# Up projection of a hybrid encoder: low and high activations as one 512-column moving operand

## What is computed

```python
h = rmsnorm(x, ffn_norm_g[l])
up = causal_dwconv(h @ w_ffn_up[l], ffn_dw_w[l], ffn_dw_b[l])   # 1024 -> 2 x 2816, width 3
gt, val = jnp.split(up, 2, axis=-1)
x = x + (jax.nn.silu(gt) * val) @ w_ffn_down[l]                 # 2816 -> 1024
...
return rmsnorm(x, final_norm_g)
```

## Time and profile before

| | us |
|---|---|
| median of 3 runs | 819.56 |
| lowest, highest | 819.24, 820.25 |
| profiled execution, its time | 820.79 |
| its span, first to last instruction | 819.0 |

### The profile page before, as it was taken

How to read it: one execution, slowest core, us unless ns; L and a number is a source line. 1 busy time by engine, 2 the same in 40 slices (tenths; PEclk the granted TensorE clock), 3 DMA queues, 4 the chain that set the end, 5 groups by cost and what they waited for, 6 DMA issues and landing times.

```text
span 819.0 us, 16096 instructions
## 1 busy us (share of the span) xinstructions
PE 803.6 (98%) x6554; PEld 777.2 (95%) x6554; DVE 585.7 (72%) x1157; ACT 520.6 (64%) x862; POOL 455.2 (56%) x139
## 2 busy tenths in 40 slices
PE   8999999999999999999999999999999999999997
PEld 8999988899999999999999999998999999999996
DVE  5799998583468875666669999885634786766655
ACT  6766798774566564555577577887546664545545
POOL 6898787787822223222288987877787024222330
PEclk9999999999999999999999999999999999999999
DMA  7654444444545555555545544444464456555441
GB/s 285 217 200 155 155 156 155 145 164 160 202 155 183 202 181 197 173 197 174 187 154 178 183 159 161 151 149 139 172 229 161 164 192 206 199 167 200 164 145 52
DMA packets 21385, 142.76 MB, mean 174 GB/s; under 512 B 2496, under 2 KB 3008, under 8 KB 4672
## 3 DMA queue, kind: packets, MB, share of 16 engines
q1 hardware_dynamic: 20736, 140.69, 49.9%
q10 hardware_dynamic: 576, 1.04, 0.3%
HBM read 140.68 MB, written 1.05 MB: 173 GB/s over the span
## 4 chain that ended last, share of the span: by engine, by line
PE 83%; ACT 7%; DVE 6%; issue 1%; DMA 1%; POOL 1%; SPq 0%; DVEq 0%; ACTq 0%
PE pu L1058 22%; PE pu L1060 22%; PE pu L1059 22%; ACT whi L319 2%; DVE pc L769 2%; DVE wlo L914 1%; PE ps L1318 1%; PE ps L1319 1%; PE ps L1320 1%; DMA x<-in_x_t 1%; PE ps L1060 1%; PE ps L1059 1%; PE ps L1058 1%; PE ps L1170 1%; ACT probs L496 1%
## 5 line engine op out<-in xcount | busy, mean ns | idle before, releaser
L261 POOL TENSOR_TENSOR wlo<-raw,whi 128x2048 fp32r<-128x2048 f32 x86 | 397.2, 4623 | 333.0 <-ACT whi L319 332.7
L1058 PE MATMUL pu<-uh,whi 128*128 128x256 f32 x880 | 249.8, 284 | 1.6 <-POOL wlo L261 1.4
L319 ACT ACTIVATE whi<-raw 128x2048 fp32r<-128x2048 f32 x129 | 245.6, 1905 | 7.9 <-PE pu L1060 7.3
L1060 PE MATMUL pu<-uh,wlo 128*128 128x256 f32 x880 | 249.0, 283 | 0.0
L1059 PE MATMUL pu<-ul,whi 128*128 128x256 f32 x880 | 249.0, 283 | 0.0
L1058 PE MATMUL pu<-hh,whi 128*128 128x256 f32 x704 | 201.7, 286 | 2.2 <-POOL wlo L261 1.4
L1060 PE MATMUL pu<-hh,wlo 128*128 128x256 f32 x704 | 199.1, 283 | 0.0
L1059 PE MATMUL pu<-hl,whi 128*128 128x256 f32 x704 | 199.1, 283 | 0.0
L1058 PEld LDWEIGHTS pu<-uh,whi 128*128 128x128 f32 x880 | 168.8, 192 | 2.4 <-issue 1.9
L1059 PEld LDWEIGHTS pu<-ul,whi 128*128 128x128 f32 x880 | 168.9, 192 | 0.4
L1060 PEld LDWEIGHTS pu<-uh,wlo 128*128 128x128 f32 x880 | 168.8, 192 | 0.0
(11 more groups left out here) (237 smaller groups left out, 1173.8 us busy)
## 6 DMA issues: line engine op xcount, KB each, us to landing
raw<-in_weights SPq DMA_DIRECT2D x130, 1024.0 KB, 4.9
raw<-in_weights SPq DMA_DIRECT2D x3, 512.0 KB, 8.9
out_y<-qk SPq DMA_DIRECT2D x3, 256.0 KB, 2.4
x<-in_x_t SPq DMA_DIRECT2D x2, 256.0 KB, 5.0
raw<-in_weights SPq DMA_DIRECT2D x2, 256.0 KB, 3.9
x<-in_x_t SPq DMA_DIRECT2D x1, 512.0 KB, 8.2
gate<-in_final_g ACTq DMA_DIRECT2D x1, 512.0 KB, 4.0
out_y<-qk ACTq DMA_DIRECT2D x1, 256.0 KB, 2.9
```

The costliest lines, as they stand in the source:

```text
L261: nc.gpsimd.tensor_tensor(wlo[s][:, :], raw[s][:, :], whi[s][:, :].bitcast(f32), ALU.subtract).then_inc(lo_ready[s], 1)
L319: A(whi[s][:, :], raw[s][:, :], ACT.Copy).then_inc(hi_ready[s], 1)
L1058: MM(out, whi[s][:, w], hi, start=start, stop=False, skip_group_check=accumulate)
L1060: return MM(out, wlo[s][:, w], hi, start=False, stop=stop, skip_group_check=accumulate)
```

## The change

`uh` and `ul` become the two halves of one tensor, `u_both`, in which high and low activations of a tile lie side by side. One matmul with 512 moving columns on the high weights (`up_products`) then makes both products with the high weights: high times high goes to the first half of a PSUM bank, high times low to the second. The product of the low weights (`up_corrections`, 256 columns) adds to the second half. So an output tile takes a whole bank, and an up unit two banks: banks 0 and 1 of the tensor `four` for even units, 2 and 3 for odd ones (before, one bank `pu` a unit; bank 3 was `po`).

After an up unit ScalarE copies the second halves of both banks to SBUF (`up_lows`), VectorE adds them to the first halves in PSUM, and then scales as before. The sums need a wait on `up_low` (ScalarE's copy) and one on `up_sum` (the add before, on the same engine). Up units do the eight high-weight matmuls of a tile ahead of its eight corrections, and wait for the low weights only between the two.

In layer 1 the four `down` banks aren't cleared: 16 transposes of `x`, ahead of the second up unit, write the residual into them as the first thing to be accumulated. `turn_x`, `keep_x_rows` and the adds of steps 4 to 7 go.

```diff
-        uh, ul = sb("uh", [P, NT, T], f32r), sb("ul", [P, NT, T], f32r)
+        u_both = sb("u_both", [P, NT, 2, T], f32r)
+        uh, ul = u_both[:, :, 0, :], u_both[:, :, 1, :]
...
-        pu = [pb(f"pu{s}") for s in range(RING)]
+        four = ctx.enter_context(nc.psum_tensor("four", [P, 4, 2, T], f32))
+        pu = [four[:, s, :, :] for s in range(RING)]
...
-        pt, po, pc = pb("pt"), pb("po"), pb("pc")
+        pt, po, pc = pb("pt"), four[:, 3, :, :], pb("pc")
+        up_lows = [gate[:, 1, 4 + 2 * ab:6 + 2 * ab, :] for ab in range(2)]
...
-                def hidden_tile(k, ab, gcol, vcol, before=None, split=None):
+                def hidden_tile(k, ab, done, gcol, vcol, before=None, split=None):
+                    act.wait_ge(*done)
+                    A(up_lows[ab], four[:, 2 * ab:2 * ab + 2, 1, :], ACT.Copy).then_inc(up_low, 1)
                     act.wait_ge(up_ready, k + 1)
...
-                    if l == DEPTH - 1 and j <= 2:
-                        keep_x_rows(j - 1)
...
-                for bank in down:
-                    last = V.memset(bank[:, :, :], 0.0)
-                last.then_inc(down_zero, 1)
+                if l < DEPTH - 1:
+                    for bank in down:
+                        last = V.memset(bank[:, :, :], 0.0)
+                    last.then_inc(down_zero, 1)
...
-                def scale_up(s, ab, done_value):
-                    dve.wait_ge(unit_done[s], done_value)
-                    V.tensor_tensor(up[:, ab, :, :], pu[s][:, :, :], rstd[:, :].unsqueeze(1).to_broadcast([P, 2, T]),
+                def scale_up(k, ab):
+                    total = four[:, 2 * ab:2 * ab + 2, 0, :]
+                    dve.wait_ge(up_low, k + 1)
+                    V.tensor_tensor(total, total, up_lows[ab], ALU.add).then_inc(up_sum, 1)
+                    dve.wait_ge(up_sum, k + 1)
+                    V.tensor_tensor(up[:, ab, :, :], total, rstd[:, :].unsqueeze(1).to_broadcast([P, 2, T]),
                                     ALU.mult).then_inc(up_ready, 1)
...
-                    if add_rows:
-                        b = j - 4
-                        dve.wait_ge(x_rows_kept, b + 1)
-                        dve.wait_ge(unit_done[1], l * USES + j + 11)
-                        V.tensor_tensor(down_rows[b], down_rows[b], x_rows[:, b, :], ALU.add).then_inc(x_rows_added, 1)
...
+                def up_products(s, first, k, m):
+                    w = slice((2 * k + m) * P, (2 * k + m + 1) * P)
+                    MM(four[:, first + m, :, :].rearrange("p a t -> p (a t)"), whi[s][:, w], u_both[:, k, :, :].rearrange("p a t -> p (a t)"),
+                       start=(k == 0), stop=False, skip_group_check=True)
+                def up_corrections(s, first, k, m):
+                    w = slice((2 * k + m) * P, (2 * k + m + 1) * P)
+                    return MM(four[:, first + m, 1, :], wlo[s][:, w], uh[:, k, :], start=False, stop=(k == NT - 1), skip_group_check=True)
+                def up_unit(s, n, first, second_free=None):
+                    pe.wait_ge(hi_ready[s], hi_count(n))
+                    for m in range(2):
+                        if m and second_free is not None:
+                            pe.wait_ge(*second_free)
+                        for k in range(NT):
+                            up_products(s, first, k, m)
+                        if m == 0:
+                            pe.wait_ge(lo_ready[s], lo_count(s, n))
+                        for k in range(NT):
+                            last = up_corrections(s, first, k, m)
+                    last.then_inc(unit_done[s], 1)
...
-                pe.wait_ge(down_zero, l + 1)
-                standard(U_FFN + 1, uh, ul)
+                pe.wait_ge(x_copied, l * 4 + 4)
+                if l < DEPTH - 1:
+                    pe.wait_ge(down_zero, l + 1)
+                else:
+                    pe.wait_ge(ul_ready, l * 12 + 8)
+                    for b in range(4):
+                        places = down[b][:, :, :].rearrange("p a (b t) -> p (a b) t", t=P)
+                        for n in range(4):
+                            MM(places[:, n, :], x[:, 4 * (b % 2) + n, P * (b // 2):P * (b // 2) + P], ident, start=(n == 0), stop=(n == 3),
+                               is_transpose=True, skip_group_check=True)
+                up_unit(1, uses(l, U_FFN + 1), 2, (rstd_ready, l * 3 + 3))
...
                     pe.wait_ge(up_ready, k - 1)
-                    unit(2, n + 10, uh, ul)
+                    up_unit(2, n + 10, 0)
                     pe.wait_ge(up_ready, k)
-                    unit(0, n + 11, uh, ul, None, {(1, 0): lambda: turn_x(j - 1)} if l == DEPTH - 1 and j <= 2 else {})
+                    up_unit(0, n + 11, 2)
```

More of the change, by code:

```diff
@@ L594, in ffn_step @@
                     col = j * 8 + PA_FW
-                    hidden_tile(k, 0, col, col + FT * 4, k - 1, lambda: split_high(l, 2, j + 11))
+                    hidden_tile(k, 0, (unit_done[2], l * USES + j + 11), col, col + FT * 4, k - 1, lambda: split_high(l, 2, j + 11))
                     act.wait_ge(unit_done[1], l * USES + j + 11)
                     hidden_high(k, 0, parity)
-                    if l == DEPTH - 1 and j <= 2:
-                        keep_x_rows(j - 1)
-                    hidden_tile(k + 1, 1, col + 4, col + FT * 4 + 4, k, None if last else lambda: split_high(l, 0, j + 12))
+                    hidden_tile(k + 1, 1, (unit_done[0], l * USES + j + 12), col + 4, col + FT * 4 + 4, k, None if last else lambda: split_high(l, 0, j + 12))
                     hidden_high(k + 1, 1, parity)
@@ L1307, in _ @@
                 scaled = parts_ready(uh_ready, l * 12 + 8, ul_ready, l * 12 + 8)
-                in_pairs(U_FFN, uh, ul, scaled)
+                def up_products(s, first, k, m):
[5 more added lines that the diff above has]
+                    return MM(four[:, first + m, 1, :], wlo[s][:, w], uh[:, k, :], start=False, stop=(k == NT - 1), skip_group_check=True)
@@ new lines, in _ @@
+                pe.wait_ge(x_copied, l * 4 + 3)
+                pe.wait_ge(hi_ready[0], hi_count(uses(l, U_FFN)))
+                pe.wait_ge(lo_ready[0], lo_count(0, uses(l, U_FFN)))
+                for p in range(NT // 2):
+                    scaled(p)
+                    places = [(k, m) for k in (2 * p, 2 * p + 1) for m in range(2)]
+                    for k, m in places:
+                        up_products(0, 0, k, m)
+                    for k, m in places:
+                        last = up_corrections(0, 0, k, m)
@@ L1320, in row_product @@
                     return MM(down_rows[b], high, wlo[s][:, w], start=False, stop=True, skip_group_check=True)
-                def turn_x(token_tile):
-                    pe.wait_ge(x_copied, l * 4 + 4)
-                    if token_tile:
-                        pe.wait_ge(x_rows_kept, 2 * token_tile)
-                    for half, bank in enumerate((po, pu[1])):
-                        places = bank[:, :, :].rearrange("p a (b t) -> p (a b) t", t=P)
-                        for n in range(4):
-                            last = nc.tensor.transpose(places[:, n, :], x[:, 4 * half + n, P * token_tile:P * token_tile + P], ident)
-                    last.then_inc(x_turned, 1)
                 def down_unit(s, k, parity):
```

23 lines of the change are left out of this document (8 added, 15 removed).

## The result

The change makes the kernel slower: 825.62 us median of 4 runs (824.39 to 827.65) against 819.77 (819.24 to 820.25), a ratio of 1.0074 [1.0052, 1.0096]. 824.0 with a range of 818 to 829 had been predicted.

A forecast was written before the change was run, and what follows sets the result against it. TensorE, 98% busy, bounds the kernel, with a second chain just holding. TensorE's 9.4 us gain is more than spent: 2.1 us late after layer 0, 2.7 in layer 1, less 0.43, sum +4.4: 824.0 us, range 818 to 829.

The forecast's parts named there:

- The sum: Whole kernel: chain and hold as worked out make it 4.4 us slower; chance 0.60 for 822 to 826.
- TensorE's gain: 44 up units: merged matmuls shorten each from 5.76 to 5.547 us, 9.4 us in all if nothing else moved.
- the wait ahead of layer 0's final down unit: End of layer 0's feed-forward stage: TensorE waits some 3.7 us, the down unit starting at 410.9.
- The second chain: Feed-forward stage: VectorE and ScalarE work from one scaling to the next; the add delays each scaling by 0.73 us.
- The waits at the start of layer 0: Layer 0's first two steps: TensorE waits 0.8, 0.4, 0.3, 1.2 and 1.0 us for the late chain.
- The hold: VectorE's L983 is held until GpSimd's split ends, in most steps; lap 16.72 us against TensorE's 16.85 in layer 0.
- it does not repeat: Rival: GpSimd does not hold L983 in later laps, lap 15.2 us, 820; chance 0.14 together with a cheaper add.
- TensorE alone: Rival: TensorE sets the end and the chain costs nothing, 810.2; chance 0.12, including most of its gain kept.
- The clock: Rival: clock falls after layer 0's 3.7 us wait, likely 827, up to 829.8; chance 0.14 with a dearer add.
- The copy: ScalarE's copy of low halves, 0.6 us with hand-over, on the chain only where a unit's end opens it.

The follow-up runs named there:

- fill: The changed kernel plus idle 512-column matmuls in two long TensorE waits (eleven in layer 0, nine in layer 1): 824.46 us, ratio 1.0055.
- pool_writes: The changed kernel with GpSimd's slot 1 split replaced, in nine steps a layer, by two fills that read nothing; output differs: 819.78 us, ratio 1.0000.
- no_add_no_copy: The changed kernel without ScalarE's copy and VectorE's add, 512-column matmuls kept; output differs: 812.28 us, ratio 0.9914.
- no_copy: The changed kernel without ScalarE's copy, VectorE's add kept and released by the unit's end; output differs: 825.30 us, ratio 1.0069.
- starts: The changed kernel with units 0 to 3 of each layer unmerged, without copy and add there: 819.04 us, ratio 0.9989.
- ends: The changed kernel with only units 20 and 21 of each layer unmerged: 824.19 us, ratio 1.0052.
- after_again: The changed kernel unaltered, measured in a second set: 826.24 us against 819.95 before, ratio 1.0076.

## Why the prediction was right, and where not

**The sum.** 4.4 us on top of before had been predicted. Without the clock's part the changed kernel takes 824.46 - 819.95 = 4.5 more (`fill`). The measured 5.9 to 6.3 are these and the clock. That the two numbers meet to 0.1 is partly luck, since the prediction over-sized TensorE's gain.

**TensorE's gain** was over-sized: 9.4 us predicted, 7.6 shown. The step that failed is the duration 0.2267 taken from the earlier trace rows, where no shorter matmuls stand between. Why a matmul there takes longer is in the last section. The error hardly reached the sum, because the chain sets the time of the last scaling and TensorE only waits less for it. For the same reason the wait ahead of layer 0's final down unit was 2.9 us from start to start (2.75 in brackets) and not 3.7: TensorE gets there later, the down unit starts at the predicted moment. It also makes TensorE's step in layer 1 16.61 instead of 16.53, so that the down units there wait 0.1 us each for GpSimd and not 0.2. The Trainium skill's fixed cost of about 2.5 ns a matmul ("TensorE: Matmul & The Clock Gate", section "Wait - 56ns, not 53.3ns?"), by which the merge would give an estimated 1.8 us, is not what the runs show: 7.6 us for 704 merges are 10.8 ns each.

**The second chain** was right in every step. Predicted, and measured (moved): add to scaling 0.73, and 0.73; the first split of GpSimd at 262.05, and 262.05; laps 16.72, and 16.71 to 16.75; layer 0's last scaling at 405.75, and 405.79; its final down unit at 410.9, and 410.95; layer 1's last scaling 3.5 late, which with layer 0's 2.1 is 808.9, and 808.92. The waits at the start of layer 0 were as put too. Added up from start to start, with the slower first matmuls behind each wait, they cost TensorE 0.86, 0.39, 0.31, 1.15 and 0.99 us, for 0.8, 0.4, 0.3, 1.2 and 1.0; the figures in the profile's brackets are smaller (0.60, 0.16, none, 0.88 and 0.76), for the reason given above. The sixth unit's corrections started at 261.97 for 261.9, step 2's down unit at 266.75 for 266.7, and step 2 ended at 271.76 (moved 272.57) for 272.45.

**The hold** repeats, at 18 of 18 splits of GpSimd. The rival "it does not repeat" had been priced at 820, and `pool_writes`, where it is taken away, gave 819.78. That the price met is partly luck: its waits, put at 10.3 us, come to some 8.4 from start to start in that run, and TensorE's gain, put at 9.4, is 7.6, so two errors of nearly the same size cancel. "TensorE alone" had been priced at 810.2, and `no_add_no_copy` gave 812.28. The rule of the Trainium skill ("SBUF - State Buffer", section "Who interferes with whom") that two SBUF inputs on VectorE and a GpSimd instruction that reads SBUF exclude each other, and that one which only writes does not, agrees with both traces: 3.14 us beside the split, 0.41 beside the memset.

**The clock** was a rival with 0.14 together with a dearer add, and it does happen, not in place of the forecast but on top. It had been placed at layer 0's final down unit, where up to 5.8 us were allowed for. There it falls, but the loss is hidden by GpSimd's split of the next unit (12.57 us against 12.56). That it would also fall behind the wait in the middle of layer 1's final down unit, where all is open, was not seen: 1.6 us. The step that failed is to have weighed the clock at one wait, when the same sum had a second wait of nearly that length in it.

**The copy** on ScalarE was rightly put at nothing within the steps. In a step's second unit it runs beside the `wlo` split. In the first it ends behind that split, by 0.6 us as predicted (VectorE waits 0.57 us for it). What the prediction didn't say in so many words is why that costs nothing: it stands ahead of the hold, as `no_copy` shows.

## What to carry to other kernels

An engine that is 98% busy isn't alone at the limit where a second chain has the same lap: here 0.73 us a unit on VectorE turned a gain of 7.6 us into a loss of 4.5, and the clock made it 6. Look for an instruction that another engine holds to its own end: as long as it starts before that end, what stands ahead of it was free to add here and worth nothing to remove, what stands behind it counted in full, and to move it into an idle gap ahead was worth 3 to 4 us with no work saved, some 2 of them without the clock's part. Such a merge pays where its extra work has slack, so it can be left out in the first and last units of a stage, and a wait of TensorE as long as these (2.3 us or more) should be priced with the clock behind it.

## What was not expected of the hardware

The granted clock fell to 0.50 at waits of TensorE of 2.30 to 2.79 us, after an otherwise unbroken stretch of work, and stayed there for 3 to 7 us; waits of 1.39 to 1.71 us left it at 1.00. It isn't the same each time. In the two traces of the changed kernel it fell 0.1 to 1.4 us after work had begun again, in `no_copy`, `starts` and `ends` while TensorE was still waiting. With a wait of 2.37 us in layer 1 it went to 0.50 in `after_again` and stayed at 1.00 in `no_copy` and `starts`. Two thirds of the changed kernel's spread go with the clock, the 2.5 us between spans of 822.6 and 825.1. The rest is time outside the span of the core's instructions, 1.8 to 3.0 us in these ten executions, and no run shows what it depends on.

A 512-column matmul of these operands starts 0.230 us after the last in blocks of eight that alternate with 256-column ones, 0.2267 in an unbroken row of them. It isn't the operands, nor each matmul of a block. The filler of `fill` has the same operands, once behind 256-column matmuls and once behind 512-column ones:

```profile
406.37 2.68 PE L1400 MATMUL four<-u_both,whi 128*128 128x512 f32 x11
...
809.80 2.20 PE L1400 MATMUL four<-u_both,whi 128*128 128x512 f32 x9
```

A single one is recorded with 0.39 us, so the starts lie (2.68 - 0.39) / 10 = 0.229 apart in the first row and (2.20 - 0.39) / 8 = 0.226 in the second. In the changed kernel's trace, too, the first five matmuls of a block of eight start 0.228 to 0.236 apart and the last three 0.2267. So it is the change from 256 to 512 columns that costs, some 27 ns each time. By that, an estimate, longer blocks would bring the merge nearer to the predicted gain; no run tried it, and why the change costs anything is open.
